# Two blocks on one core: three more weight buffers for the experts, filled early, and an opening in one stage

## The reference

```
for l in range(2):
    mod_lat = silu(c) @ ada_w[l] + ada_b[l]            # shifts, scales, gates from one vector
    h = rms_norm(x, norm_mix_g[l]) * (1 + scale) + shift
    x = x + g1 * mixer[l](h)
    h = rms_norm(x, norm_ffn_g[l]) * (1 + scale2) + shift2     # 512 rows in layer 0, 256 in layer 1
    scores = sigmoid(h @ router_w); best group of 4 experts, best 2 in it; w = scores / their sum
    for e in range(16):
        y = y + comb[:, e] * ((silu(h @ w1[e]) * (h @ w3[e])) @ w2[e])
    x = x + g2 * y
```

## Time and profile before

| | |
|---|---|
| median of 3 runs | 2713.39 us (2712.89 to 2716.74) |
| the profiled execution | 2711.09 us |
| its span, first to last instruction | 2709.3 us |
| PE busy | 2453.9 us (91%) |
| DVE, ACT, POOL busy | 836.2, 465.0, 113.2 us |
| opening, to the mixer's first product | 0 to 52.34 us |
| experts of layer 0, first to last product | 526.45 to 834.8 us |
| experts of layer 1, first to last product | 1052.43 to 1344.0 us |
| second block | from 1363.94 us |

### The profile page before, as it was taken

One profiled execution on the slowest core, in us unless ns is written; L12 is line 12 of the kernel. 1 busy time (PEld: TensorE's weight loads), 2 busy tenths in 40 slices (PEclk: granted clock), 3 DMA queues, 4 the chain that ended last, 5 costly groups with the idle time before them and its releaser, 6 DMA issues.

```text
span 2709.3 us, 29559 instructions
## 1 busy us (share of the span) xinstructions
PE 2453.9 (91%) x11656; PEld 1629.7 (60%) x11656; DVE 836.2 (31%) x2095; ACT 465.0 (17%) x991; POOL 113.2 (4%) x170
## 2 busy tenths in 40 slices
PE   5999999599974886977689999999999999999999
PEld 3455654334322353322247888888884888888884
DVE  0246331410103453000024874122200677412220
ACT  2133331211102222100011121011101112201110
POOL 0000000000001001000000004000000000400000
PEclk8999999799997997998889999999999999999999
DMA  7413288289996305999845333444443543343442
GB/s 248 131 37 89 85 302 317 84 291 370 380 388 250 103 15 191 370 381 380 303 154 170 127 125 132 149 151 148 146 145 113 167 144 125 125 155 125 155 148 101
DMA packets 299320, 509.30 MB, mean 188 GB/s; under 512 B 25840, under 2 KB 118640, under 8 KB 299184
## 3 DMA queue, kind: packets, MB, share of 16 engines
q1 hardware_dynamic: 281936, 473.88, 50.3%
q0 software_dynamic: 4864, 17.04, 2.0%
q10 hardware_dynamic: 12384, 16.51, 1.7%
HBM read 492.45 MB, written 14.94 MB: 187 GB/s over the span
## 4 chain that ended last, share of the span: by engine, by line
PE 81%; DMA 10%; DVE 4%; ACT 2%; issue 1%; ACTq 1%; DVEq 1%; SPq 0%; POOL 0%; POOLq 0%
PE bank L2478 34%; DMA ring<-in_exp_w 9%; PE bank L670 4%; PE bank L2464 4%; PE bank L704 4%; PE bank L1464 3%; PE bank L1474 3%; PE bank L2598 3%; PE bank L2613 3%; PE bank L1851 2%; PE bank L337 2%; PE bank L1953 2%; PE bank L680 1%; PE bank L2572 1%; PE bank L2562 1%
## 5 line engine op out<-in xcount | busy, mean ns | idle before, releaser
L2478 PE MATMUL bank<-hT,ring 128*128 128x256 f32 x3456 | 759.9, 380 | 7.1 <-DVE hT L2804 7.1
L2478 PEld LDWEIGHTS bank<-hT,ring 128*128 128x128 f32 x3456 | 652.7, 190 | 97.0 <-issue 10.4
L670 PE MATMUL bank<-ring,hg 128*64 128x512 f32 x1024 | 247.8, 628 | 38.1 <-DMA ring<-in_exp_w 31.5
L2919 DVE SCALAR_TENSOR_TENSOR y_conf<-y_glu,s_cw,y_conf 128x256 f32<-128x256 f32 x480 | 195.0, 478 | 0.8
L670 PEld LDWEIGHTS bank<-ring,hg 128*64 128x64 f32 x1024 | 76.0, 143 | 179.0 <-issue 165.6
L704 PE MATMUL bank<-ring,hidA 128*64 128x512 f32 x512 | 135.6, 678 | 44.0 <-DMA ring<-in_exp_w 39.3
L842 DVE TENSOR_TENSOR hidA<-sgT,bank 128x256 f32<-128x256 f32 x32 | 13.5, 422 | 463.0 <-ACT sgT L796 290.8
L3001 DVE SCALAR_TENSOR_TENSOR y_conf<-bank,s_fw,y_conf 128x255 f32<-128x255 f32 (+1 forms) x176 | 72.7, 475 | 212.9 <-ACT y_conf L2747 211.3
L2464 PE MATMUL bank<-ring,hT 128*128 128x512 f32 (+1 forms) x320 | 119.1, 535 | 6.6 <-DVE hT L2804 6.6
L704 PEld LDWEIGHTS bank<-ring,hidA 128*64 128x64 f32 x512 | 39.5, 154 | 133.5 <-issue 133.5
L1464 PE MATMUL bank<-ring,hT 128*128 128x384 f32 (+2 forms) x256 | 97.8, 525 | 2.9 <-ACTq L134 2.9
(11 more groups left out here) (450 smaller groups left out, 2646.7 us busy)
## 6 DMA issues: line engine op xcount, KB each, us to landing
ring<-in_exp_w SPq DMA_DIRECT2D x192, 1024.0 KB, 10.6
ring<-in_ada_w SPq DMA_DIRECT2D x24, 2048.0 KB, 8.3
ring<-in_w_in SPq DMA_DIRECT2D x24, 2048.0 KB, 7.7
ring<-in_w_up SPq DMA_DIRECT2D x44, 1024.0 KB, 6.7
ring<-in_w_in SPq DMA_DIRECT2D x32, 1024.0 KB, 7.8
ring<-in_w_down SPq DMA_DIRECT2D x8, 2048.0 KB, 7.9
moe_y<-ye ACTq DMA_DIRECT2D x72, 128.0 KB
ring<-in_w_attn_out SPq DMA_DIRECT2D x4, 2048.0 KB, 7.9
```

The source lines that it names most:

```text
L670: mm = pe.matmul(bank[2][SA * a:SA * a + SA, :], hg[:, e % 2, kk, 0:SA], w[a][:, k, :], start=(kk == 0), stop=(kk == KT - 1))
L2478: mm = pe.matmul(b, w[:, k, j * P:(j + 1) * P], moving(k), start=(k == 0), stop=(k == KT - 1))
L2919: ins = dve.scalar_tensor_tensor(conf[:, f, :], src, cw[:, f, k:k + 1], conf[:, f, :], ALU.mult, ALU.add)
```

## The change

Three things are changed.

**Buffers.** `chunk_buffers` takes three more buffers of 2 MB (`EXTRA = 3`) in each of the two layers. The experts use six: the three new ones and then the ring (`N_BUF = 6`). SP fills all six before the expert loop; the new three carry chunks 0 to 2 and need no mixer chunk to be used first, only that their memory is done with (`extra_free`: in layer 0 the end of the stage with heads and attention, in layer 1 the start of the layer). The sixth chunk belongs to the third expert, so experts 0, 1 and 2 are now fixed (`FIXED = 3`).

**Memory.** What the even mixer kept in memory of its own (`omix`, `bias`, `va`, `pT`) lies in the new buffers; the experts' rows (`hs`, `hg`, `yg`) lie in `hT` and `h_tok`, which nobody reads by then. One expert place of layer 0 is narrower, 64 rows in place of 96.

**Opening.** Turning and writing `hT` are part of the stage with the products; the writes are split between ACT and DVE. Nine of ACT's loads go to SP, behind the fourth chunk of `ada_w`, and `router_w_wide` is laid out so that a partition reads one run.

```diff
-WIDTHS = [[128] * 4 + [96] * 6 + [64] * 6, [96] * 4 + [64] * 12]
+WIDTHS = [[128] * 4 + [96] * 5 + [64] * 7, [96] * 4 + [64] * 12]
+FIXED = 3
+EXTRA = 3
...
-        load(act, params_landed,
+        load(act, mod_params_landed,
              [(gcols[:, :, 0, :], A["norm_mix_cols"].rearrange("l p k -> p l k")),
               (gcols[:, :, 1, :], A["norm_ffn_cols"].rearrange("l p k -> p l k")),
-              (bcols[:, :, :], A["ada_b_cols"].rearrange("l p k -> p l k")),
-              (router_w[:, :, :], rows(A["router_w_wide"])),
...
+              (bcols[:, :, :], A["ada_b_cols"].rearrange("l p k -> p l k"))])
...
             first.stream(0, 4)
+
+            @block.sync
+            def _(sp):
+                load(sp, params_landed,
+                     [(router_w[:, :, :], A["router_w_wide"].rearrange("p (k n) -> p k n", k=KT)),
...
             @st.scalar
             def _(act):
                 act.wait_ge(cond_landed.sem, cond_landed.n)
                 act.activation(silu_c[:, :, 0:2], cond[:, :, :], ACT.Silu).then_inc(silu_ready.sem, 1)
+                first.copy(act, 0)
                 act.wait_ge(x_landed.sem, x_landed.n)
-                on_scalar(act)
-                for f in range(4):
+                for m in range(4):
+                    act.activation(xn[:, m, :], x[:, m, :], ACT.Square, accum_out=stats[:, 0, m:m + 1])
...
+                for f in range(1, 4):
                     first.copy(act, f)
+                act.wait_ge(rows_scaled.sem, r0 + MODS_READY)
+                for k in (0, 1, 2, 6):
+                    act.wait_ge(bank_full.sem, f0 + k + 1)
+                    for cond_no, lo in ((1, 0), (0, CT * P)):
+                        act.activation(hT[:, k, lo:lo + 2 * P], bank[k][:, lo:lo + 2 * P], ACT.Identity,
+                                       scale=modc[0][:, KT + k, cond_no:cond_no + 1], bias=modc[0][:, k, cond_no:cond_no + 1])
...
             @st.vector
             def _(dve):
-                on_vector(dve)
-                dve.wait_ge(params_landed.sem, params_landed.n)
-                for f in range(4):
-                    first.keep(dve, f, [0])
+                dve.wait_ge(mod_params_landed.sem, mod_params_landed.n)
+                first.keep(dve, 0, [0])
+                dve.wait_ge(act_out.sem, a0 + 1)
+                dve.reciprocal(stats[:, 2, 0:4], stats[:, 1, 0:4])
...
+                for k in (3, 4, 5, 7):
+                    dve.wait_ge(bank_full.sem, f0 + k + 1)
...
             @block.sync
             def _(sp):
 
-                for j in range(RING):
-                    used, value = used_at[n0 + j - RING]
-                    sp.wait_ge(used.sem, value)
+                sp.wait_ge(stage_done.sem, extra_free)
+                for j in range(N_BUF):
+                    if j >= len(extra):
+                        used, value = used_at[n0 + j - len(extra) - RING]
+                        sp.wait_ge(used.sem, value)
                     load_weights(sp, j, slice(order[j][1], order[j][1] + 1))
...
-            hs = sb(mem, f"hs{l}", [P, 2, D])
-            hg = sb(mem, f"hg{l}", [P, 2, KT, P])
+
+            hs = hT[:, 0:4, :].rearrange("p k t -> p (k t)").rearrange("p (b d) -> p b d", b=2)
+            hg = hT[:, 4:8, :].rearrange("p k t -> p (k t)").rearrange("p (b k s) -> p b k s", b=2, k=KT)
...
-                        which_was, e_was, half_was = order[(j - RING) % n_w]
-                        back = 0 if j >= RING else 1
+                        which_was, e_was, half_was = order[(j - N_BUF) % n_w]
+                        back = 0 if j >= N_BUF else 1
...
-            pool.memset(tie[:, 0:1], 2.0 ** 17)
-            pool.memset(tie[:, 1:2], 2.0 ** 16)
+            for e in range(FIXED):
+                pool.memset(tie[:, e:e + 1], (FIXED - e) * 2.0 ** 17)
...
-            omix = sb(mem, "omix", [P, 4, D])
+
+            omix = extra[0][:, :].rearrange("p (i d) -> p i d", i=4)
+            bias = extra[1][:, :].rearrange("p (t h s) -> p t h s", t=LT, h=H_A)
+            va = extra[2][:, 0:2048].rearrange("p (i d) -> p i d", i=4)
+            pT = extra[2][:, 2048:4096].rearrange("p (j d) -> p j d", j=4)
```

196 lines of the change are left out of this document (93 added, 103 removed).

## The result

The changed kernel took **2671.97 us** (median of 4 runs, 2667.46 to 2672.36); the kernel before, measured beside it, 2714.46 (4 runs, 2712.89 to 2716.74). The ratio is 0.984, with a 95% interval of 0.9824 to 0.9855: 1.6% faster. The forecast was 2671, its range 2656 to 2686.

The account below looks back on a forecast made before the run. PE is busy 91% of the span, but transfers bound the ends of the expert loops; 17.2 + 16.8 + 8.3 = 42.3 us off 2711.1 gives 2668.8, plus 2.3 for the median: 2671 us, range 2656 to 2686.

Parts of the forecast that it names:

- Layer 0: Layer 0's expert loop: three chunks less to come, 16.5 us, plus 0.7 for narrower transfers; 17.2 us, bounds 11 and 32.
- Layer 1: Layer 1's expert loop: DMA-bound from 1080 on, so 6.29 MB at 374 GB/s save 16.8 us; bounds 11 and 20.
- Price of a chunk: Layer 0's expert loop: one 2.097 MB weight chunk takes 5.50 us at 381 GB/s.
- The earlier loads and the new places in memory: Before the expert loops: extra loads hide in DMA gaps and moved buffers add no wait; cost nothing.
- rival B: Expert loops, L655: gathers wait behind the deeper weight backlog; slower, 2760 us; chance 0.03.
- The opening: Start to the mixer's first product: it begins at 44.0 in place of 52.34, 8.3 us gained; bounds 4 and 11.3.
- Rival A: More than the sum: mixer's first products at high clock, 6.8 us, or layer 0 nearer PE's floor; 2656 to 2662; chance 0.13.
- The narrower place: Layer 0's tenth expert place: PE saves 6.2 us, all under the DMA's bound, so nothing; transfers save 0.7 us.
- D: Less than the sum: opening gives 4, each layer 11; 2687 us; chance 0.14 including results between it and the forecast.
- E: New chunks aren't ahead, only the opening gains: 2705 us; chance 0.07 including results between it and D.
- The sum: Whole kernel: 17.2 + 16.8 + 8.3 = 42.3 us gained.
- What would show it: Profile signs: weight waits 70.8 to about 37 us, loops about 291 and 275, gathers about 7, first mixer product at 44.

Follow-up runs that it names:

- once: Changed kernel with the three extra buffers filled before the loop but used once only, then the ring's three alone: 2705.18 us, ratio 0.9976 to before.
- late: Changed kernel with six buffers, but the three extra ones loaded only after the expert loop's first product: 2681.18 us, ratio 0.9878 to before.
- ring3: Changed kernel with the three extra buffers unused, experts' weights going through the ring's three alone: 2705.07 us, ratio 0.9965 to before.
- wide9: Changed kernel with layer 0's tenth expert place back at 96 rows: 2673.49 us, ratio 0.9851 to before.
- before_again: The kernel before, unchanged, profiled a second time: 2709.79 us.
- old_open: Changed kernel with the opening of before (two stages, nine loads on ACT), keeping the new router weight layout: 2677.87 us, ratio 0.9862 to before.
- before_layout: The kernel before with only the new layout of the router's weights: 2707.84 us, ratio 0.9986 to before.

## Why the prediction was right, and where it wasn't

**Layer 0, 17.2 us forecast: 16.4.** The size was right. The working gave two reasons: "three chunks that are in memory before the loop starts are three chunks less to come", and that the DMA "stands up to five chunks ahead in place of two". The first is false by itself (`once`: nothing), the second carries most of the gain (`late`: 14.4 of 16.4). I had both on the page and took the sum from the first; since each comes to three chunks, the number couldn't tell them apart. By the last landing, which is what was worked out, it is 18.1. The 0.7 us for the narrower place's transfers isn't told apart: the last landing is the same before and in `ring3` (302.9), and 1.4 us later in `wide9` than in the changed kernel.

**Layer 1, 16.8: 17.7.** The size was right again; the step "nothing but bytes counts" was wrong: bytes without depth give 1.2 us by the last landing, depth without bytes 4.4, both 16.2. The 1.5 us between 16.2 and the loop's 17.7 lie behind the last landing (8.7 us before, 7.2 after), where the level of the clock decides: luck, as `before_again` shows, with 5.4 us there. The reader could have seen it in the two stretches of before above, where the engines idle in layer 1's wide places too (0.66 and 0.87). I read from 1080 on, where they no longer do.

**Price of a chunk, 5.5 us: 5.2** over five chunks of layer 1, and 6.0 over three of layer 0 (18.1 by the last landing).

**The earlier loads and the new places in memory, nothing (within 1 us): 1 to 2 us in layer 0's mixer.** With routing it took 475.0 us against 474.1, and 475.7 in `ring3` without any earlier load, so that the surplus isn't the loads'. It took 474.1 in `before_again` too, 474.3 in `old_open`, which has the opening of before, and 474.8 to 476.7, in the mean 475.5, in the nine executions with another opening. What these 1.4 us are stays open. The way to layer 1's loop is 217.3 against 217.6.

**Gathers (rival B): no.** They land in 6.8 us against 6.9 in the earlier trace rows, PE's two waits for them are 11.5 us against 11.4, though the weights in front of them now take 15 to 16. By the round robin that the Trainium skill describes (DMA: Bandwidth & Descriptors, Queues, rings and completion order) this is what should happen, and the trace now agrees also for the deeper queue.

**The opening, 8.3: 9.2** in the profiled pair, 9.9 between the means of two and of seven executions. The timeline of products, turns and writes came as worked out (43.1 against 44.0), though a part of that is luck: the same code began the mixer at 39.8 to 43.1. What was wrong is the weight of its first sentence, that ACT can do nothing before its list is out: undone, it costs about 2 us, which is within the scatter, because PE waits for `ada_w` (12.3, then 4.4 us) in any case. The new layout of the router's weights had no term of its own and is worth about 3 us where the loads stay on ACT; with them on SP it isn't told apart here.

**Rival A (clock high at the mixer's start): no.** The first products took 1.89 us for eight at 43.10, at the lower level as before. The reason given against it, PE's idle time while `hT` is written (3.17 us), isn't enough by itself: in `before_layout` PE idled 3.15 us there, and its first two groups of eight ran at the higher level (1.06 and 1.04 us), the rest at the lower (1.87); its first 14 us had a granted clock of 0.57 in place of 0.50, and its mixer with routing took 472.4 us. In the other twelve executions they began at the lower level. Layer 0 didn't reach PE's floor either: PE still waits 17.5 us for weights there.

**The narrower place, nothing: nothing** (`wide9`). **D and E** are out by the two loops' lengths.

**The sum.** 16.4 + 17.7 + 9.2 = 43.4 came in, 42.3 was forecast; the mixer's 0.9 and the second block's 3.8 us were given back in the profiled pair, 0.4 came from small pieces: 39.0. Against the medians, 2714.46 - 2671.97 = 42.5. A part of the exactness is luck: executions of one kernel differ by 5 us and more.

**What would show it.** Right: both loops' lengths, the DMA share in the saturated stretches, the gathers, the opening. Wrong: "PE's waits for experts' weights fall from 70.8 to about 37". They fell to 58.5, those of layer 0 to 17.5 and not below 10. The step that failed is to equate time saved with waits saved. Of the 34.1 us that the two loops lost, 12.3 were these waits; 21.6 were PE's busy time (10.1 and 11.5). Of these, 6.2 are the narrower place by the sum of its products' times (4.3 by `wide9`), which I had costed at nothing for the time: under a bound by transfers, work taken from PE turns into waits (`wide9`: 4.6 us of them), and so by my own sum the waits should have ended 6 us higher. The other 15 to 17 us are products that ran at the higher clock level, sixteen of them in 3.65 us in place of 5.35. Part of this is scatter between executions: `before_again` has 78.1 us of waits for weights and 9.5 us less busy time in the two loops than the first execution. Over the three executions of before and its variant (70.8, 78.1, 79.9) and the four that have the changed kernel's loops (58.5, 59.4, 58.7, 55.6) the waits fell by 18 us. The rest is the narrower place and the clock.

## What to carry to other kernels

In a loop that starts compute-bound and ends transfer-bound, as these two do, more buffers help by the lead that the transfers have at the turn; look for idle transfer engines ahead of it. Prefetching into buffers without more depth can be worth nothing: the lead is lost while no buffer is free. In a loop bound by transfers judge a change by when the last chunk lands, not by PE's waits: PE's slack stands partly in waits and partly in products at the lower clock.

## What was not expected of the hardware

- The same 1344 matmuls of layer 1's loop took 240.0 and 232.2 us in two executions of the kernel before (granted clock 0.91 and 0.94), with the last landing after 282.9 and 283.0 us: with the transfers as the bound, PE's clock moved its busy time by 8 us and the end of the loop by 3.
- A load of many small pieces can hold up the issuing of the loads behind it: with the router's weights in eight runs of 128 bytes for each partition, two later loads took 4.85 and 4.93 us to issue; in one run of 1 KB, the first took 0.46 and the second still 4.45. What the 4.45 us wait for isn't shown.
- The opening of one and the same code ended between 39.8 and 43.1 us, and the second block of one and the same code took 1345.4 to 1352.2 us, both along with the clock that was granted; pieces should be compared over several executions where a few microseconds matter.
